# Moving the prompt's value product behind four groups of transposes in an attention stage

## The chip, the core and the metric

The kernel runs on one core of a Trainium2 chip. The metric is the device time of one launch in microseconds (us). Smaller is better. TensorE is PE in the profile, and its weight loads are listed apart as PEld; VectorE is DVE, ScalarE is ACT, GpSimd is POOL, and SP is the engine whose queue issues most transfers.

## What is computed

One inference step of a two-layer decoder: a recurrent layer (retention and a gated linear recurrence), then an attention layer, each with a SwiGLU block behind it. 1024 prompt positions and 8 samples of 8 new positions go through it together. The change lies in the attention of the second layer, which does two things:

```python
# prompt: 16 heads, 128 positions a block, keys of three dilated windows combined
s = q @ k.T * Dh ** -0.5 - slope * distance        # banded, per head
p = exp(s - max(s));  den = sum(p)
o = (p @ v) / den
# samples: 8 x 8 queries against 2048 cached keys and values of each sample, gathered by stride,
# and against the 8 new ones; same softmax, same combination
```

## The kernel before

**Slots.** The attention stage is a software pipeline of slots n, written out in one order for every engine. A slot is one block of 128 prompt queries of one pair of heads: 8 pairs (`HP`) times 8 blocks (`QT`), n = 0 to 63. In slot n TensorE makes the scores of block n (`scores(n)`, L2419), the transposes of the probabilities of block n - 1, and the value product of block n - 2 (`pv(n - 2)`, L2501 and L2505). The later the block in its pair (n % 8), the wider its scores (128 to 1024 keys) and the more there is to transpose.

**The samples ride along.** Eight slots carry one sample b: its step is s = (n + 5) % 8, so the last sample but its tail ends at slot 55. Steps 0 to 5 transpose ten tiles of cached keys (L2444) and multiply each by the sample's queries (`tile_scores`, L2472), step 6 transposes the sample's probabilities, and step 7 takes the sample's value product (L2526, L2523).

**Turns.** A group of transposes is a turn: usually four 128x128 blocks that fill one PSUM bank, then one copy out of the bank by ACT (cached keys, L2561) or DVE (probabilities, L2638). A cached key tile takes two turns. `TURN_BANK` gives four banks, numbered 0 to 3; a table made ahead of time, `TB_`, gives each turn the bank that was used longest ago of those allowed. Banks 2 and 3 are the second halves of the score banks. Where the scores of a slot are wider than 512 keys (n % 8 of 4 or more), these two are not allowed in parts 1 and 2 of the slot. `turn` waits on `t_out` until the bank's last content has been copied out.

**Parts of a slot.** A slot has four parts f. Part 1 holds the scores and turns 0 and 1, part 2 turns 2 and 3, part 3 turns 4 and 5, part 4 the rest. `SCORED` says behind which part each key tile is multiplied: tile 0 behind part 2 of step 0, tile 1 behind part 3 of step 0, tiles 2 and 3 likewise in step 1, tile 4 behind part 2 of step 2, tile 7 behind part 2 of step 4. Those four tiles behind part 2 (0, 2, 4, 7) are all made from turns 0 and 1 of the slot or from earlier ones.

For the four steps concerned the first four turns and their banks are:

```
step 0 (n % 8 = 3): key, key, key, key             banks: four different ones
step 1 (n % 8 = 4): key, key, key, key             banks: 1, 0, 1, 0
step 2 (n % 8 = 5): key, key, key, probabilities   banks: 1, 0, 1, 0
step 4 (n % 8 = 7): key, key, key, probabilities   banks: 1, 0, 1, 0
```

**The other engines.** ACT in a slot: copies out key turns 0 and 1, exponential of the first head's scores (L2585), key turn 2, exponential of the second head, key turn 3, then the row of reciprocal denominators that `pv` left in PSUM (L2607). DVE: scores plus bias with their maxima (L2679), the reciprocal (L2684), the copies of the probability turns (L2638) and of the sample's scores (L2653) in TensorE's order, last the output of `pv` times that row (L2710, semaphore `a_ox`), for which the next `pv` waits, as both use one bank. POOL makes the diagonal matrix for `pv` (L2765) and issues the loads of q, k, v and bias. SP loads the cached tiles, each buffer as soon as the turns or products that read it have run.

Of the kernel before, what the change touches and what calls it, by code (L numbers as in the profile page):

```python
# [132 lines left out]
def build(nc, a):  # L133
# [2121 lines left out]
    def slot_of(b, s):  # L2255

        return LAST_S.get(s, 8 * b + s - LEAD) if b == DB - 1 else 8 * b + s - LEAD

    def sample_slot(n):
        b, s = divmod(n + LEAD, 8)  # L2260
        if n >= min(LAST_S.values()) or b >= DB or slot_of(b, s) != n:
            b, s = DB - 1, next((s for s, x in LAST_S.items() if x == n), None)
        return (b, s) if s is not None else (None, None)

    K_AT = (0, 4, 8, 11, 14, 17, 20, 20, 20)
    SCORED = {(0, 2): (0,), (0, 3): (1,), (1, 2): (2,), (1, 3): (3,), (2, 2): (4,), (3, 1): (5,), (3, 3): (6,), (4, 2): (7,),
              (5, 1): (8,), (5, 3): (9,)}
    WEIGHED = {(7, 1): range(1, 5), (7, 2): range(5, 8), (7, 4): (8, 9, 10, 0)}

    def turns(n):  # L2270

        units = []
        b, s = sample_slot(n)
        if n == -LEAD:
            units += [("qs", 0, 0), ("ks", 0, 0)]
        if b is not None:
            units += [("k", i // 2, i % 2) for i in range(K_AT[s], K_AT[s + 1])]
        if -LEAD < n <= 2 - LEAD:
            units += [("qk", 0, 2 * (n + LEAD - 1) + i) for i in range(2)]
        elif 0 <= n < NSLOT - QT and n % QT in (1, 2):  # L2280
            units += [("qk", n // QT + 1, 2 * (n % QT - 1) + i) for i in range(2)]
        if n == slot_of(DB - 1, 7) + 3:
            units += [("out", 0, 0), ("out", 1, 0)]
        if s == 6:
            units += [("s", b, z) for z in range(3)]
        if 1 <= n <= NSLOT:
            units += [("p", n - 1, k) for k in range(0, 2 * ((n - 1) % QT + 1), 4)]
        return units
# [5 lines left out]
    def phase(n, f):  # L2294

        nt = len(turns(n))
        return range(2 * f - 2, min(2 * f, nt) if f < 4 else nt)
# [40 lines left out]
    def tile_used(j):  # L2338

        b, u = divmod(j, 20)  # L2340
        if u < 10:
            s = max(i for i in range(8) if K_AT[i] <= 2 * u + 1)
            n = 8 * b + s - LEAD
            return n, max(i for i, x in enumerate(turns(n)) if x[0] == "k" and x[1] == u)
        s, f = [x for x, steps in WEIGHED.items() if u - 9 in steps][0]
        return slot_of(b, s), 20 * f + u
# [54 lines left out]
    def att_pe(pe):  # L2401
        def scores(n):
            p, qb = divmod(n, QT)
            W = (qb + 1) * P
            if n:
                pe.wait_ge(a_red, 2 * n)
            else:
                pe.wait_ge(v_out, NT * N_QKV)
            if qb == 0:
                bank, count = qk_last(p)  # L2410
                pe.wait_ge(t_out[bank], count)
            for c in range(0, W, 512):
                if c:
                    for x in (2, 3):
                        if turns_before(n, x):
                            pe.wait_ge(t_out[x], turns_before(n, x))
                for i, (q, k) in enumerate(((QH, KH), (QH, KL), (QL, KH))):
                    for e in range(2):
                        mm = pe.matmul(PS[:, 2 * e + c // 512, 0:min(512, W - c)],  # L2419
                                       q[p % 2][e * DH:(e + 1) * DH, qb * P:(qb + 1) * P],  # L2420
                                       k[p % 2][e * DH:(e + 1) * DH, c:min(W, c + 512)], start=(i == 0), stop=(i == 2))
            mm.then_inc(a_s, 1)
# [53 lines left out]
        def tile_scores(b, t):  # L2476
            bank, count = k_last(b, t)
            pe.wait_ge(t_out[bank], count)
            if t == 0:
                pe.wait_ge(b_qb, 5 * (b + 1) + 2 if b else 6)  # L2480
                if b:
                    pe.wait_ge(b_o4, b)
            elif t % 2 == 0:
                pe.wait_ge(b_red, 6 * b + t // 2 + 1)
            mm = sample_scores(lambda hp: SKT[:, t % 2, hp, :], (t % 2) * P, P)
            if t == 1:
                mm = sample_scores(lambda hp: KNB[:, hp, :], 2 * P, DS)
            if t % 2:
                mm.then_inc(b_sc, 1)

        def pv(m):
            p, qb = divmod(m, QT)
            bank, count = last_turn(m + 1, "p", m)
            pe.wait_ge(t_out[bank], count)
            if qb == 0:
                pe.wait_ge(a_vl[p % 2], 16 * (p // 2 + 1))
            if m:
                pe.wait_ge(a_ox, m)
            for x in range(qb + 1):
                for e in range(2):  # L2500
                    pe.matmul(PS[e * DH:(e + 1) * DH, 6, 0:P], VN[p % 2][:, x, e * DH:(e + 1) * DH],  # L2501
                              PT[:, m % 2, e * (qb + 1) + x, :], start=(x == 0), stop=(x == qb), tile_position=(0, e * DH))
            pe.wait_ge(a_dg, m + 1)
            for e in range(2):
                mm = pe.matmul(PS[e * DH:(e + 1) * DH, 6, P:2 * P], ones[:, 0:DH], ADG[:, m % 2, e, :],  # L2505
                               start=True, stop=True, tile_position=(0, e * DH))
            mm.then_inc(a_o, 1)

        def sample_pv(b, steps):
            for i in steps:  # L2510
                t = i - 1
                j = 20 * b + 10 + t
                if i == 1:
                    for bank, count in last_turns(slot_of(b, 6), "s", b):
                        pe.wait_ge(t_out[bank], count)
                if i == 0:
                    pe.wait_ge(b_vn if b else b_v0, 16 * max(b, 1))
                else:
                    pe.wait_ge(b_tile[BUF[j]], load_due(j))
                for g in range(4):  # L2520
                    c = slice(256 * g, 256 * (g + 1))
                    if i == 0:
                        mm = pe.matmul(PS[NQ * g:NQ * (g + 1), 7, 256:512], PTS[0:DS, NTL, NQ * g:NQ * (g + 1)], VNB[:, c],  # L2523
                                       start=False, stop=True, tile_position=(0, NQ * g))
                    else:
                        mm = pe.matmul(PS[NQ * g:NQ * (g + 1), 7, 256:512], PTS[:, t, NQ * g:NQ * (g + 1)], TILE[BUF[j]][:, c],  # L2526
                                       start=(i == 1), stop=False, tile_position=(0, NQ * g))
                if i != NTL:
                    mm.then_inc(b_vu, 1)

        def step(n, f):
            b, s = sample_slot(n)
            if 0 <= n < NSLOT and f == 1:
                scores(n)
            for i in phase(n, f):
                turn(n, i)
            if 2 <= n and f == 1:
                pv(n - 2)
            for t in SCORED.get((s, f), ()):
                tile_scores(b, t)  # L2540
            sample_pv(b, WEIGHED.get((s, f), ()))

# [443 lines left out]
```

## Time and profile before

| | |
|---|---|
| median of 3 runs | 2783.97 us (2781.9 to 2784.48) |
| profiled execution: its own time | 2784.42 us |
| its span | 2782.6 us |
| PE busy, share of the span | 2739.0 us, 98% |
| PEld busy | 2618.6 us, 94% |
| DVE busy | 1737.1 us, 62% |
| ACT busy | 946.1 us, 34% |
| granted TensorE clock, mean | 0.998 of full speed |

The profile is one execution. The attention slots run from about 1504 to 1929 us. In rows of the timeline, the first column is the start in us from the span's start and the second the length; equal instructions are merged, with their number behind the x. In square brackets stands the idle time of the engine ahead of the row, and what ended it; "issue" means that the profile shows nothing that it waited for. Most fp32 matmuls are two instructions in the trace, a transpose is one. A 128*64 ahead of a shape is the part of the array used, rows by columns.

### The profile page before, as it was taken

How to read it: one execution, taken by the hardware profiler on the slowest of the kernel's cores; microseconds unless marked ns; L12 is line 12 of the kernel's file. 1: busy time of each engine (PE TensorE's matmuls, PEld its weight loads, DVE VectorE, ACT ScalarE, POOL GpSimd, SP SyncE). 2: the span in 40 equal slices, each digit the busy share in tenths (PEclk: the TensorE clock that was granted, in tenths of full speed). 3: DMA queues.
4: the chain of work that ended last, by engine and by line, in shares of the span. 5: the costliest groups of instructions: out<-in, count | busy, mean ns of one | idle time of the engine just before them, and what ended most of it. 6: DMA issues, size and time to landing. Idle time of an engine off the chain costs nothing.

```text
span 2782.6 us, 54662 instructions
## 1 busy us (share of the span) xinstructions
PE 2739.0 (98%) x23577; PEld 2618.6 (94%) x23577; DVE 1737.1 (62%) x2858; ACT 946.1 (34%) x1690; POOL 118.5 (4%) x220
## 2 busy tenths in 40 slices
PE   7999999999999999999999999999999999999998
PEld 7999999999999999999997777777999999999998
DVE  5754536877777776755512566556377767776676
ACT  5543513322222222422223555555232222222222
POOL 1010000000000000000011111110000000000000
PEclk9999999999999999999999999999999999999999
DMA  5120220111111111232356776873101111111112
GB/s 200 37 80 18 67 92 30 32 60 47 47 46 46 46 46 47 85 112 85 95 176 212 237 258 220 266 253 129 61 16 46 46 46 47 46 47 46 53 55 80
DMA packets 126381, 254.53 MB, mean 91 GB/s; under 512 B 7617, under 2 KB 88725, under 8 KB 125632
## 3 DMA queue, kind: packets, MB, share of 16 engines
q1 hardware_dynamic: 112944, 189.26, 21.0%
q0 software_dynamic: 11888, 57.25, 5.9%
q8 instruction: 189, 3.10, 0.5%
q10 hardware_dynamic: 1312, 4.52, 0.5%
q14 instruction: 48, 0.39, 0.0%
HBM read 222.98 MB, written 28.02 MB: 90 GB/s over the span
## 4 chain that ended last, share of the span: by engine, by line
PE 92%; DVE 4%; ACT 2%; DMA 1%; issue 1%; POOL 0%; ACTq 0%; POOLq 0%; DVEq 0%
PE psum L1574 30%; PE psum L1629 17%; PE psum L483 14%; PE psum L224 11%; PE psum L1549 3%; PE psum L2444 3%; PE psum L2501 2%; PE psum L2419 2%; PE psum L2459 2%; PE psum L2472 1%; PE psum L2526 1%; DMA x_natural<-in_x_prompt 1%; DMA cache_tile<-in_cache_k 1%; PE psum L592 1%; PE psum L2448 1%
## 5 line engine op out<-in xcount | busy, mean ns | idle before, releaser
L1810 DVE TENSOR_TENSOR x_res<-x_res,psum 128x544 f32<-128x544 f32 x352 | 250.5, 719 | 155.5 <-PE psum L1629 155.5
L483 PE MATMUL psum<-w_hi,h_hi 128*128 128x256 f32 (+1 forms) x1152 | 327.2, 284 | 1.0 <-ACT qkv_tok L2074 1.0
L483 PE MATMUL psum<-w_hi,h_lo 128*128 128x256 f32 (+1 forms) x1152 | 323.6, 281 | 0.0
L483 PE MATMUL psum<-w_lo,h_hi 128*128 128x256 f32 (+1 forms) x1152 | 323.0, 280 | 0.0
L1629 PE MATMUL psum<-ffn_hi,ffn_unit_hi 128*128 128x272 f32 x1408 | 292.6, 289 | 1.8 <-DVE x_res L1810 1.5
L1629 PE MATMUL psum<-ffn_lo,ffn_unit_hi 128*128 128x272 f32 x1408 | 291.5, 288 | 0.0
L1629 PE MATMUL psum<-ffn_hi,ffn_unit_lo 128*128 128x272 f32 x1408 | 290.7, 288 | 0.0
L1574 PE MATMUL psum<-h_hi,ffn_unit_lo 128*128 128x272 f32 x1280 | 265.2, 288 | 0.0
L1574 PE MATMUL psum<-h_lo,ffn_unit_hi 128*128 128x272 f32 x1280 | 264.8, 288 | 0.0
L1574 PE MATMUL psum<-h_hi,ffn_unit_hi 128*128 128x272 f32 x1280 | 264.5, 288 | 0.0
L1629 PEld LDWEIGHTS psum<-ffn_hi,ffn_unit_hi 128*128 128x128 f32 x1408 | 220.7, 188 | 3.2 <-DVE x_res L1810 3.2
L1629 PEld LDWEIGHTS psum<-ffn_lo,ffn_unit_hi 128*128 128x128 f32 x1408 | 220.8, 188 | 0.0
L1629 PEld LDWEIGHTS psum<-ffn_hi,ffn_unit_lo 128*128 128x128 f32 x1408 | 220.7, 188 | 0.0
L483 PEld LDWEIGHTS psum<-w_hi,h_hi 128*128 128x128 f32 (+1 forms) x1152 | 215.1, 187 | 4.6 <-issue 2.2
L483 PEld LDWEIGHTS psum<-w_lo,h_hi 128*128 128x128 f32 (+1 forms) x1152 | 215.2, 187 | 0.0
L483 PEld LDWEIGHTS psum<-w_hi,h_lo 128*128 128x128 f32 (+1 forms) x1152 | 215.0, 187 | 0.0
L1574 PEld LDWEIGHTS psum<-h_hi,ffn_unit_hi 128*128 128x128 f32 x1280 | 201.0, 188 | 0.0
L1574 PEld LDWEIGHTS psum<-h_hi,ffn_unit_lo 128*128 128x128 f32 x1280 | 200.7, 188 | 0.0
L1574 PEld LDWEIGHTS psum<-h_lo,ffn_unit_hi 128*128 128x128 f32 x1280 | 200.6, 189 | 0.0
L1574 PE MATMUL psum<-ffn_t_hi,ffn_unit_lo 128*128 128x272 f32 x960 | 198.6, 288 | 0.0
L1574 PE MATMUL psum<-ffn_t_hi,ffn_unit_hi 128*128 128x272 f32 x960 | 198.6, 288 | 0.0
L1574 PE MATMUL psum<-ffn_t_lo,ffn_unit_hi 128*128 128x272 f32 x960 | 198.5, 288 | 0.0
(385 smaller groups left out, 5307.1 us busy)
## 6 DMA issues: line engine op xcount, KB each, us to landing
cache_tile<-in_cache_k SPq DMA_DIRECT2D x64, 512.0 KB, 8.5
cache_tile<-in_cache_v SPq DMA_DIRECT2D x64, 512.0 KB, 11.9
w_raw<-in_w_ffn_gate SPq DMA_DIRECT2D x22, 1024.0 KB, 5.1
w_raw<-in_w_ffn_up SPq DMA_DIRECT2D x22, 1024.0 KB, 5.1
w_raw<-in_w_ffn_down SPq DMA_DIRECT2D x22, 1024.0 KB, 4.9
w_raw<-in_w_in_att SPq DMA_DIRECT2D x12, 1024.0 KB, 7.1
w_raw<-in_w_in_rec SPq DMA_DIRECT2D x10, 1024.0 KB, 5.0
park_x<-x_res POOLq DMA_DIRECT2D x2, 4368.0 KB, 13.3
```

What stands on the lines that cost most here:

```text
L224: mm = pe.matmul(PS[:, bank + c, 0:n], st[slot][:, wc:wc + P], mv[:, k, c * CW:c * CW + n], start=(i < NCH), stop=(i >= 3 * NCH * nk - NCH))
L483: mm = pe.matmul(PS[0:n, bank, 0:BW], st[:, k, w:w + n], mv[slot][:, k * BW:(k + 1) * BW], start=(k == 0 and x == 0) if used is None else ...
L592: pe.matmul(PS[:, bank, 0:n], wt[:, j, :], XC[j % 2][:, c * CW:c * CW + n], start=True, stop=True).then_inc(g_in, 1)
L1549: mm = pe.matmul(PS[:, 2 * s + c, 0:CC], st[slot][:, k * BW + f * P:k * BW + (f + 1) * P], mv[:, k, t * TH + c * CC:t * TH + (c + 1) * CC] ...
L1574: mm = pe.matmul(PS[:, 2 * s + c, 0:CC], st[i % NU][:, k * P:(k + 1) * P], mv[:, k0 + k, t * TH + c * CC:t * TH + (c + 1) * CC], start=(fr ...
L1629: mm = pe.matmul(PS[:, 2 * s + c, 0:CC], st[(w0 + m // 2) % NU][:, x:x + P], mv[:, f, t * TH + c * CC:t * TH + (c + 1) * CC], start=(n < 2 ...
L1810: dve.tensor_tensor(x, x, pset(dset(g, i)), ALU.add).then_inc(s_res, 1)
L2419: mm = pe.matmul(PS[:, 2 * e + c // 512, 0:min(512, W - c)], q[p % 2][e * DH:(e + 1) * DH, qb * P:(qb + 1) * P], k[p % 2][e * DH:(e + 1) * ...
L2444: mm = pe.transpose(to[:, h * P:(h + 1) * P], TILE[BUF[j]][:, hp * P:(hp + 1) * P], ident[:, :])
L2448: mm = pe.transpose(to[:, t * P:(t + 1) * P], (QN, KN)[c // 2][:, 4 * (c % 2) + t, :], ident[:, :])
L2459: mm = pe.transpose(to[:, (k - c) * P:(k - c + 1) * P], SX[x % 2][:, e, y * P:(y + 1) * P], ident[:, :])
L2501: pe.matmul(PS[e * DH:(e + 1) * DH, 6, 0:P], VN[p % 2][:, x, e * DH:(e + 1) * DH], PT[:, m % 2, e * (qb + 1) + x, :], start=(x == 0), stop ...
```

## The change

In steps 0, 1, 2 and 4 of a sample `pv(n - 2)` is issued in part 2 of the slot, behind turns 2 and 3 and directly ahead of the product of a key tile, in place of part 1, behind turns 0 and 1. In all other slots it stays in part 1. No instruction is added or taken out, and the order on the other engines and in the bank table stays.

```diff
     SCORED = {(0, 2): (0,), (0, 3): (1,), (1, 2): (2,), (1, 3): (3,), (2, 2): (4,), (3, 1): (5,), (3, 3): (6,), (4, 2): (7,),
               (5, 1): (8,), (5, 3): (9,)}
+    PV_AT = {0: 2, 1: 2, 2: 2, 4: 2}
     WEIGHED = {(7, 1): range(1, 5), (7, 2): range(5, 8), (7, 4): (8, 9, 10, 0)}
...
                 scores(n)
             for i in phase(n, f):
                 turn(n, i)
-            if 2 <= n and f == 1:
+            if 2 <= n and f == PV_AT.get(s, 1):
                 pv(n - 2)
             for t in SCORED.get((s, f), ()):
                 tile_scores(b, t)
```

Sample 0 has these steps in slots below 0, where there is no `pv`. Samples 1 to 7 have them in slots 3 to 55, four each, 28 slots in all.

## Rows read from the trace of the kernel before

**Rows 1.** The page: engine totals, and the chain that ended last.
```profile
PE 2739.0 (98%) x23577; PEld 2618.6 (94%) x23577; DVE 1737.1 (62%) x2858; ACT 946.1 (34%) x1690; POOL 118.5 (4%) x220
...
PE 92%; DVE 4%; ACT 2%; DMA 1%; issue 1%; POOL 0%; ACTq 0%; POOLq 0%; DVEq 0%
```

**Rows 2.** Waits of PEld, 1526 to 1830 us: total us, times, longest.
```profile
PEld psum L2444 <- issue: 14.9, 54, 2.9
...
PEld psum L2472 <- ACT smp_kt L2561: 2.9, 12, 0.3
PEld psum L2419 <- DVE att_pt L2638: 2.8, 6, 0.5
```

**Rows 3.** Waits of PE, same stretch.
```profile
PE psum L2444 <- DMA cache_tile<-in_cache_k: 2.5, 1, 2.5
```

**Rows 4.** Timeline of PEld, slot 12 (step 1).
```profile
1587.25 0.85 PEld L2444 LDWEIGHTS psum<-ident,cache_tile 128*128 128x128 f32 x8
1588.27 0.64 PEld L2501 LDWEIGHTS psum<-att_pt,att_v 128*64 128x64 f32 x12 [0.17 <-issue]
...
1589.30 0.85 PEld L2444 LDWEIGHTS psum<-ident,cache_tile 128*128 128x128 f32 x8 [0.17 <-issue]
1590.32 0.38 PEld L2472 LDWEIGHTS psum<-smp_kt,smp_q_blocks 128*32 128x32 f32 x16 [0.17 <-issue]
1590.89 0.85 PEld L2459 LDWEIGHTS psum<-ident,att_scores 128*128 128x128 f32 x8 [0.20 <-issue]
1591.93 0.38 PEld L2472 LDWEIGHTS psum<-smp_kt,smp_q_blocks 128*32 128x32 f32 x16 [0.18 <-ACT smp_kt L2561]
```

**Rows 5.** Timeline of ACT, slot 12.
```profile
1587.94 1.09 ACT L2561 ACTIVATE smp_kt<-psum 128x512 f32<-128x512 f32 x2 [2.43 <-PE psum L2444]
...
1589.99 0.60 ACT L2561 ACTIVATE smp_kt<-psum 128x512 f32<-128x512 f32 x1 [0.16 <-PE psum L2444]
...
1591.29 0.59 ACT L2561 ACTIVATE smp_kt<-psum 128x512 f32<-128x512 f32 x1
```

**Rows 6.** Timeline of PEld, slot 14: value product, key tile, 16 transposes, key tile.
```profile
1602.17 0.25 PEld L2505 LDWEIGHTS psum<-att_diag,ones 128*64 128x64 f32 x4
1602.59 0.38 PEld L2472 LDWEIGHTS psum<-smp_kt,smp_q_blocks 128*32 128x32 f32 x16 [0.17 <-issue]
1603.17 0.42 PEld L2444 LDWEIGHTS psum<-ident,cache_tile 128*128 128x128 f32 x4 [0.20 <-issue]
...
1605.07 0.14 PEld L2472 LDWEIGHTS psum<-smp_kt,smp_q_blocks 128*32 128x32 f32 x5 [0.17 <-issue]
```

**Rows 7.** Timeline of PEld, slot -1: three key turns, two banks, no value product.
```profile
1501.65 0.89 PEld L2444 LDWEIGHTS psum<-ident,cache_tile 128*128 128x128 f32 x8
1503.04 0.42 PEld L2444 LDWEIGHTS psum<-ident,cache_tile 128*128 128x128 f32 x4 [0.49 <-ACT smp_kt L2561]
```

**Rows 8.** Timeline of ACT, slot -1.
```profile
1502.39 1.08 ACT L2561 ACTIVATE smp_kt<-psum 128x512 f32<-128x512 f32 x2
```

**Rows 9.** Timeline of PEld, slot 11 (step 0): its first turn and its second key tile.
```profile
1581.03 0.86 PEld L2444 LDWEIGHTS psum<-ident,cache_tile 128*128 128x128 f32 x8 [0.36 <-issue]
...
1585.39 0.38 PEld L2472 LDWEIGHTS psum<-smp_kt,smp_q_blocks 128*32 128x32 f32 x16 [0.30 <-ACT smp_kt L2561]
```

**Rows 10.** Timeline of ACT, slot 11: key turn 3.
```profile
1584.76 0.58 ACT L2561 ACTIVATE smp_kt<-psum 128x512 f32<-128x512 f32 x1
```

**Rows 11.** Timeline of ACT, slot 15 (step 4): its last copy.
```profile
1612.25 0.26 ACT L2607 ACTIVATE att_rden_rows<-psum 128x128 f32<-128x128 f32 x1
```

**Rows 12.** Timeline of DVE, slot 15: end of its queue.
```profile
1612.22 1.62 DVE L2638 COPY att_pt<-psum 128x512 f32<-128x512 f32 x3
1613.76 0.28 DVE L2710 TENSOR_TENSOR att_out<-psum,att_rden_rows 128x128 f32<-128x128 f32 x1
```

**Rows 13.** Timeline of PEld: first turns of slot 15, value product of slot 16.
```profile
1607.22 0.86 PEld L2444 LDWEIGHTS psum<-ident,cache_tile 128*128 128x128 f32 x8 [0.36 <-issue]
...
1614.27 1.51 PEld L2501 LDWEIGHTS psum<-att_pt,att_v 128*64 128x64 f32 x28 [0.17 <-issue]
```

## The prediction

> **What bounds the kernel now.** I read the page first. PE is busy for 98% of the span and makes up 92% of the chain that ended last [rows 1], so whatever adds to or takes from PE's line of work should show in the time, unless PE waits for something later in the same slot. Next I asked what PE waits for in the attention slots. From 1526 to 1830 us one wait is for a transfer, 2.5 us [rows 3], and it lies ahead of the first moved product (slot 3's first turn). The waits for DVE are six of at most 0.5 us, and those for ACT are 12 of at most 0.3 us [rows 2]. The rest of PEld's idle time is put down to issue: some 0.2 us each time PE goes from full-width transposes to a product on a part of the columns or back [rows 2, 4]. PE is therefore nearly always behind its own work, and the slot's length is the sum of its PE groups plus these gaps. The reader should see in the timeline that a slot is a ladder: turns, gap, value product, gap, turns, gap, key tile, gap, turns.
>
> **What the change moves.** Nothing is added. In 28 slots the value product goes from between turns 1 and 2 to behind turn 3. I work it out from the start of turn 0 to the start of turn 4, for slot 12. Let V stand for the whole value product to the next group's start (1589.30 - 1588.27 = 1.03 us); it has the same length in both places, since the step from a value product to a key tile takes as long as that to a transpose: from L2505's first load to the next group it is 1602.59 - 1602.17 = 0.42 us [rows 6], with an idle of 0.17 us in either case [rows 4, 6].
>
> *Before* [rows 4]: turns 0 and 1 take 1588.27 - 1587.25 = 1.02 us, gap included; V; turns 2 and 3 take 1590.32 - 1589.30 = 1.02 us; the key tile takes 1590.89 - 1590.32 = 0.57 us. Sum 2.61 us + V.
>
> *After, if no bank holds PE up*: 16 transposes in a row (4 at 1603.17 and 12 behind them) with one gap take 1605.07 - 1603.17 = 1.90 us [rows 6], then V, then 0.57 us. Sum 2.47 us + V. That saves 0.14 us a slot: one gap out of four goes.
>
> *After, with the banks as they are* (steps 1, 2 and 4): turn 2 takes the bank of turn 0, and turn 3 that of turn 1. Today V lies between, and ACT has emptied both banks by 1587.94 + 1.09 = 1589.03, ahead of turn 2 at 1589.30 [rows 4, 5]. This cover goes. ACT begins the first copy 1587.94 - 1587.25 = 0.69 us after turn 0 starts, and ends both at 0.69 + 1.09 = 1.78 us. How long PE takes to go on behind a copy can be read in slot -1, which has just this order: the copies begin at 1502.39, one lasts about 0.60 us [rows 5], and turn 2 starts at 1503.04, so 0.05 us behind it, after 0.49 us of idle [rows 7, 8]. So turn 2 starts at 0.69 + 0.60 + 0.05 = 1.34 us and runs 0.42 us to 1.76. Turn 3 waits for the second copy and starts at 1.78 + 0.05 = 1.83 us. With its own 0.42 us and the gap of 0.17 us, V starts at 2.42 us. The sum is 2.42 + 0.57 = 2.99 us + V, against 2.61 us + V: **0.38 us longer** in each such slot. Put otherwise, 0.52 us of waiting is new and 0.14 us of gap is saved.
>
> Steps 2 and 4 have a probability turn as turn 3, but in the bank of turn 1, so the same copy by ACT gates it. Over all 21 slots of these three steps ACT starts its first copy 0.69 or 0.70 us after turn 0, and the two pairs of turns take 1.02 or 1.03 us each; the longer value products of steps 2 and 4 are part of V and cancel. 21 x 0.38 = 8.0 us.
>
> *Step 0* (7 slots) has four different banks, so its turns 2 and 3 don't wait, and 0.14 us is saved up to turn 4. But the slot's next key tile (tile 1) needs turn 3's copy, which ACT makes behind both exponentials: it ends at 1584.76 + 0.58 = 1585.34, and PE starts the tile at 1585.39 after 0.30 us of idle, against the 0.17 us it would have anyway [rows 9, 10]. This 0.13 us of waiting grows by what PE gained. ACT is held there by its own queue and DVE's maxima, not by the transposes. So step 0 is worth 0; if ACT moved forward too, it would be -0.14 x 7 = -1.0 us.
>
> **What hides the rest, and what is late next.** ACT's copies of turns 2 and 3 stand behind its exponentials: in slot 12 turn 3's copy ends at 1591.29 + 0.59 = 1591.88 and PE reaches tile 3 at 1591.93 with almost nothing to spare [rows 4, 5]. After the change PE comes there 0.38 us later, so this does not add. The value product's own result comes later, at 2.42 us + V in place of 1.02 us + V. ACT copies its denominator row last in the slot: in slot 15, at 1612.25 [rows 11]. There the product would have ended some 2.42 + 1.68 us after 1607.22 [rows 13] (1.68 us is V for its 24 + 4 instructions), at about 1611.3, so 0.9 us ahead of ACT, and ACT is not held. DVE's output comes last too, at 1613.76 behind its copies, and these wait for turns that all move by the same 0.38 us [rows 12]. POOL's diagonal is made in the slot before, or early in it. SP's loads of key tiles are released by turns 2 and 3, which come 2.05 - 1.34 = 0.7 us earlier in the slot; the one transfer wait stands ahead of all of it [rows 3], so this buys nothing.
>
> In slot 14 and its like PE waits up to 0.5 us for DVE's copy of a probability turn [rows 2]. That copy follows turns 4 and 5 of slot 13, which the change delays as much as the scores behind them, so the wait stays and doesn't soak up the 0.38 us.
>
> **The sum.** 21 x 0.38 + 7 x 0 = +8.0 us. The profiled execution took 2784.42 us, so it would become 2792.4 us; it lies 0.45 us above the median of the runs, and the median would become 2792.0 us (+0.29%). Against 0.2% (5.6 us), about what a measurement of this kernel tells from no change, this is slower, with not much room.
>
> **Bounds.** For the wait: nothing, as all other engines' work in these slots is hidden, up to what slot -1 shows, where turn 2 starts 1.39 us after turn 0 and not 1.34; if both waits had 0.05 us more, a slot would lose 0.48 us, or 10.1 us in all. At the low end step 0's gain is kept: 7.0 us. For lower ones see the rivals.
>
> **What a page says.** The Trainium skill, TensorEngine Tiling (Array Packing), section Key Properties, says that changing the tiling mode drains TensorE, while changing the tile alone doesn't. The trace agrees as far as it goes: the idle of 0.17 to 0.20 us stands where the part of the array changes (128*128, 128*64, 128*32) and not between transposes of two kinds [rows 4, 6]. By this rule alone the change saves one of four switches in 28 slots, and the kernel gets faster; that is the first rival, and it is worked out there from rows.
>
> **Rivals.**
> 1. *The saved switch decides (faster).* If ACT freed the banks in time, each slot would gain its gap, up to 0.17 us [rows 4]: 28 x 0.17 = 4.8 us, so 2779.2 us. For this, ACT would have to end its two copies about 0.5 us earlier than it does, by 1.25 us after turn 0's start in place of 1.78. It starts at 0.69 us in every slot, with turn 0 only just finished, and is idle ahead of that (2.43 us [rows 5]), so it can't start earlier. Chance 0.05.
> 2. *The wait is absorbed (no change that shows).* The new wait would be given back where PE waits anyway: DVE's copy of the slot behind step 2 (0.50 - 0.17 = 0.3 us, 7 times, 2 us) if DVE, which can take step 2's first probability turn earlier, came through sooner, and step 0's 1.0 us. Then 8.0 - 3.0 = +5.0 us, 2789.0 us. Against it, the copy starts when the turn is done and not when DVE is free. Chance 0.10.
> 3. *The late value product adds a wait of its own (slower still).* Its output would reach DVE late, and the next slot's product, which waits for the bank, would stand. The tightest is step 4: DVE's output ends at 1614.04 [rows 12] and the next product's first load stands at 1614.27 [rows 13]. If ACT's row slipped past its place by 0.3 us in each of the 21 slots, it would add 6 us: 2798 us. The 0.9 us of slack above speaks against it. Chance 0.06.
>
> **How the numbers follow.** The forecast, with its bounds of 7.0 to 10.1 us, has 0.79. From these bounds alone the range would be 2791.0 to 2794.1 us; with a scatter of the median of 1 to 2 us (the runs shown lie 2.6 us apart), 2789.5 to 2795.5 us. To leave out no more than 2 in 10, the range takes in rival 2 partly: 2788.0 to 2795.5 us. Slower by over 0.2% (above 2789.5 us): the forecast and rival 3, 0.84. Within 0.2%: rival 2 and the forecast's lower edge, 0.11. Faster: rival 1, 0.05.
>
> **What would show it in the profile after.** In slots of steps 1, 2 and 4, sixteen transposes ahead of L2501 with two idles of PEld put down to ACT smp_kt L2561: about 0.5 us ahead of turn 2 and less than 0.1 us ahead of turn 3, together some 11 us over 21 slots. From turn 0 to turn 4 slot 12 should take 3.64 + 0.38 = 4.02 us. In step 0, no idle ahead of turn 2, and tile 1 still at 4.36 us behind turn 0, its idle up from 0.30 to about 0.44 us. L2444's gaps put down to issue should fall by about 28 x 0.17 us. The forecast is wrong if the wait at turn 2 is absent, if ACT starts its copies sooner, or if new waits of L2501 on att_out or of L2505 on att_diag appear.

## The result and the profile after

The changed kernel took 2790.84 us (median of 13 runs, 2788.95 to 2792.08), the kernel before 2784.56 us in its 13 runs beside it. The ratio is 1.0022, with a 95% interval of 1.0015 to 1.0029: some 6.1 us slower, between 4.2 and 8.1 us. The forecast was +8.0 us, 2792.0 us, with a range of 2788.0 to 2795.5 us. Of the 27 runs of the kernel before that stand beside the last four experiments, one took 9802.58 us and is left out of their ratios. The changed file has one line more above the attention code, so L2444 of before is L2445 now, and so on.

The page of the kernel after, engine totals, and the chain that ended last, by line:

```profile
span 2788.4 us, 54662 instructions
...
PE 2740.0 (98%) x23577; PEld 2618.5 (94%) x23577; DVE 1737.4 (62%) x2858; ACT 943.7 (34%) x1690; POOL 118.8 (4%) x220
...
PE psum L1574 30%; PE psum L1629 17%; PE psum L483 14%; PE psum L224 11%; PE psum L1549 3%; PE psum L2502 2%; PE psum L2445 2%; PE psum L2420 2%; PE psum L2460 2%; PE psum L2473 2%; PE psum L2527 1%; ACT smp_kt L2562 1%; DMA x_natural<-in_x_prompt 1%; PE psum L592 1%; PE psum L2449 1%
```

The work is the same to within 1 us on PE, PEld, DVE and POOL, and 2.4 us less on ACT [rows 1]; the span is 5.8 us longer. The chain now names ACT's copy of the cached keys (`smp_kt`), which is not among the fifteen entries on the page of the kernel before. The waits of PEld from 1526 to 1838 us say where it stands:

```profile
PEld psum L2445 <- issue: 10.3, 30, 2.5
PEld psum L2473 <- issue: 9.4, 55, 0.2
PEld psum L2445 <- ACT smp_kt L2562: 8.8, 18, 0.5
...
PEld psum L2420 <- DVE att_pt L2639: 2.8, 6, 0.5
...
PEld psum L2473 <- ACT smp_kt L2562: 1.5, 5, 0.3
```

Against [rows 2]: the cached keys' transposes (L2445) have 24 gaps put down to issue less (54 to 30), and a new wait on ACT, 18 times 0.49 us (this stretch holds 18 of the 21 slots). The wait for DVE's copies is unchanged, 2.8 us.

Slot 12 (step 1), the timeline of PEld and under it that of ACT, to be laid beside [rows 4, 5]:

```profile
1588.50 0.85 PEld L2445 LDWEIGHTS psum<-ident,cache_tile 128*128 128x128 f32 x8
1589.84 0.91 PEld L2445 LDWEIGHTS psum<-ident,cache_tile 128*128 128x128 f32 x8 [0.49 <-ACT smp_kt L2562]
1590.92 0.63 PEld L2502 LDWEIGHTS psum<-att_pt,att_v 128*64 128x64 f32 x12 [0.17 <-issue]
...
1591.94 0.38 PEld L2473 LDWEIGHTS psum<-smp_kt,smp_q_blocks 128*32 128x32 f32 x16 [0.17 <-issue]
1592.52 0.86 PEld L2460 LDWEIGHTS psum<-ident,att_scores 128*128 128x128 f32 x8 [0.20 <-issue]
1593.54 0.38 PEld L2473 LDWEIGHTS psum<-smp_kt,smp_q_blocks 128*32 128x32 f32 x16 [0.17 <-issue]
```
```profile
1589.19 1.09 ACT L2562 ACTIVATE smp_kt<-psum 128x512 f32<-128x512 f32 x2 [2.43 <-PE psum L2445]
...
1590.98 0.60 ACT L2562 ACTIVATE smp_kt<-psum 128x512 f32<-128x512 f32 x1
...
1592.27 0.60 ACT L2562 ACTIVATE smp_kt<-psum 128x512 f32<-128x512 f32 x1
```

ACT starts its first copy 1589.19 - 1588.50 = 0.69 us behind turn 0, as before. Turn 2 follows 1.34 us behind turn 0. The second group of eight loads takes 0.91 us and not 0.85: the small wait ahead of turn 3 lies inside it. It is too short to be listed as idle, so the second of the two idles that the forecast named does not appear as a row. The value product starts at 2.42 us, and turn 4 at 1592.52 - 1588.50 = 4.02 us. All three are the numbers of the forecast.

Slot 11 (step 0), PEld, then ACT:

```profile
1582.43 1.73 PEld L2445 LDWEIGHTS psum<-ident,cache_tile 128*128 128x128 f32 x16 [0.36 <-issue]
1584.33 0.42 PEld L2502 LDWEIGHTS psum<-att_pt,att_v 128*64 128x64 f32 x8 [0.17 <-issue]
...
1585.71 0.64 PEld L2460 LDWEIGHTS psum<-ident,att_scores 128*128 128x128 f32 x6 [0.20 <-issue]
1586.64 0.38 PEld L2473 LDWEIGHTS psum<-smp_kt,smp_q_blocks 128*32 128x32 f32 x16 [0.29 <-ACT smp_kt L2562]
```
```profile
1584.72 0.20 ACT L2586 ACTIVATION_READ_ACCUMULATOR att_scores<-att_scores,att_max 128x1 f32 x1
1584.81 0.59 ACT L2562 ACTIVATE smp_kt<-psum 128x512 f32<-128x512 f32 x1
...
1585.99 0.60 ACT L2562 ACTIVATE smp_kt<-psum 128x512 f32<-128x512 f32 x1
```

The same slot before, turn 4:

```profile
1584.46 0.64 PEld L2459 LDWEIGHTS psum<-ident,att_scores 128*128 128x128 f32 x6 [0.20 <-issue]
```

Sixteen transposes run through without a wait, and turn 4 starts 1585.71 - 1582.43 = 3.28 us behind turn 0, in place of 1584.46 - 1581.03 = 3.43 us [rows 9]: the saved gap is 0.15 us. But tile 1 comes earlier too: it starts 1586.64 - 1582.43 = 4.21 us behind turn 0, and the forecast had it stay at 4.36 us [rows 9].

From the starts of the scores one can take the length of every slot in both traces. Slots 0 to 3, 45, 50, 51 and 53 hold pauses or waits of other kinds and are set aside (last section). In the others the differences, after less before, are these, the same within 0.02 us from sample to sample:

| step | forecast, us a slot | trace, us a slot |
|---|---|---|
| 0 | 0.00 | -0.15 |
| 1 | +0.38 | +0.36 |
| 2 | +0.38 | +0.39 |
| 4 | +0.38 | +0.37 |
| 3, 5, 6, 7 | 0.00 | 0.00 (within 0.01) |

Times seven samples, that is 7 x 0.97 = +6.8 us. The two profiled spans differ by less, 5.8 us. The rest lies in the slots set aside and ahead of slot 0 (last section).

Slot 3, the first with a moved product, is one of those set aside. PE waits there for a cached key tile, 2.5 us before and 2.1 us after, standing idle, and then runs for a few us at a lower granted clock: the mean between 1528 and 1530 us is 0.62 before and 0.50, the lower level of 1.2 GHz, after. All 16 transposes ahead of the moved product take 3.17 us there, in place of 1.73 us in slot 11.

### The profile page after: what moved, and what is told of

It reads as the page before. It is cut to its first block, busy times and chain, and to the rows that moved or that the text cites. A ratio compares the mean times of both kernels' runs of the same rounds, so it can differ in the third digit from the quotient of the medians.

```text
span 2788.4 us, 54662 instructions
## 1 busy us (share of the span) xinstructions
PE 2740.0 (98%) x23577; PEld 2618.5 (94%) x23577; DVE 1737.4 (62%) x2858; ACT 943.7 (34%) x1690; POOL 118.8 (4%) x220
## 4 chain that ended last, share of the span: by engine, by line
PE 92%; DVE 4%; ACT 3%; DMA 1%; issue 1%; POOL 0%; ACTq 0%; POOLq 0%; DVEq 0%
PE psum L1574 30%; PE psum L1629 17%; PE psum L483 14%; PE psum L224 11%; PE psum L1549 3%; PE psum L2502 2%; PE psum L2445 2%; PE psum L2420 2%; PE psum L2460 2%; PE psum L2473 2%; PE psum L2527 1%; ACT smp_kt L2562 1%; DMA x_natural<-in_x_prompt 1%; PE psum L592 1%; PE psum L2449 1%
```

## The experiments

A difference "a slot" is always against the kernel before, taken from the starts of the scores as above, in the samples that hold no such pause. The medians of the first four experiments stand beside 2784.01 us for the kernel before, those of the last four beside 2784.27 us. The ratios differ from the quotient of the two medians by up to 0.0006. Lines that a diff leaves out are marked by "..."; `PV_AT = {0: 2}` and the short copies are shown against the changed kernel, ACT's new order against the run ahead of it, the others against the kernel before.

### The move in step 0 alone

```diff
-    PV_AT = {0: 2, 1: 2, 2: 2, 4: 2}
+    PV_AT = {0: 2}
```

> The product moves in step 0 alone (7 slots, four different banks, so no wait for a bank). Theory A, read from the profile after: the third key copy of ACT starts 0.15 us sooner there because its transposes come sooner, the rest of ACT's chain follows, and each of the 7 slots gets 0.15 us shorter: -1.0 us in all, about 2783.5 us against 2784.6, and no wait on ACT ahead of turn 2. Theory B, as the prediction had it: tile 1 is held by ACT anyway, the slots keep their length, 0.0 us. The time can hardly tell them apart, the starts of the slots in the trace can (5.93 us from slot 11 to slot 12 before, by B the same, by A 5.78).

Measured: 2784.22 us against 2784.01 us, ratio 0.9999 (0.9991 to 1.0008), no difference that the time can tell. The trace can: five samples have step 0 shorter by 0.14 or 0.15 us, every other step without a pause is within 0.02 us. Slot 27, PEld:

```profile
1688.79 1.73 PEld L2445 LDWEIGHTS psum<-ident,cache_tile 128*128 128x128 f32 x16 [0.37 <-issue]
...
1693.00 0.38 PEld L2473 LDWEIGHTS psum<-smp_kt,smp_q_blocks 128*32 128x32 f32 x16 [0.30 <-ACT smp_kt L2562]
```

Again 4.21 us and not 4.36. Theory A holds, and the forecast's zero for step 0 does not. The reason can be seen in ACT's timeline of slot 11 in the kernel before, in two rows that the forecast did not use:

```profile
1583.32 0.20 ACT L2585 ACTIVATION_READ_ACCUMULATOR att_scores<-att_scores,att_max 128x1 f32 x1
1583.56 0.60 ACT L2561 ACTIVATE smp_kt<-psum 128x512 f32<-128x512 f32 x1
```

The third copy starts 0.24 us behind the row ahead of it. Where only ACT's own queue holds such a copy it starts 0.09 us behind (1584.72 to 1584.81 after the change). It was waiting for turn 2's transposes, for too short a time to be listed as idle. They come sooner now, the copy starts 2.38 us behind turn 0 in place of 2.53, and everything behind it on ACT moves along, tile 1 too. From there ACT's own queue holds the copy, so these 0.15 us are all that a slot of step 0 can gain while ACT keeps its order. That PE's saved gap is 0.15 us as well is a coincidence; the run with two tiles side by side, further down, tells the two apart.

### The tile moved up to the product

The product stays behind turn 1, and tiles 0, 2, 4 and 7 are multiplied directly behind it, in samples 1 to 7. `scored` takes the place of `SCORED.get((s, f), ())` on PE and DVE, here and in every later run whose edit names `EARLY`.

```diff
+    EARLY = {0: 1, 2: 1, 4: 1, 7: 1}
+
+    def scored(b, s, f):
+        if not b:
+            return SCORED.get((s, f), ())
+        return [t for (x, g), ts in SCORED.items() for t in ts if x == s and EARLY.get(t, g) == f]
...
-            for t in SCORED.get((s, f), ()):
+            for t in scored(b, s, f):
```

> Product and key tile stand side by side as in the changed kernel, but the tile moves up to the product (behind turn 1), not the product down to the tile. Theory A (ACT's copies decide, a change of array part costs 0.15 us): no wait for a bank ahead of turn 2, but turns 2 and 3 come 0.57 us later. In steps 0 and 1 ACT's third copy waits for them, and with it the second key tile: +0.6 us and +0.57 us a slot. In step 2 DVE's copies come a little late for the second half of the next scores: +0.1. In step 4 nothing waits: -0.14. Sum 7 x 1.1 = +8 us, 2792.5 us. Theory C (it is the neighbourhood that pays, and the loss came from moving the product late): every one of the 28 slots gets 0.14 us shorter, -4 us, 2780.6 us.

Measured: 2792.59 us, ratio 1.0028 (1.0016 to 1.0039). Slot 28 (step 1), PEld, then ACT:

```profile
1698.89 0.86 PEld L2451 LDWEIGHTS psum<-ident,cache_tile 128*128 128x128 f32 x8
...
1700.94 0.38 PEld L2479 LDWEIGHTS psum<-smp_kt,smp_q_blocks 128*32 128x32 f32 x16 [0.17 <-issue]
1701.52 0.86 PEld L2451 LDWEIGHTS psum<-ident,cache_tile 128*128 128x128 f32 x8 [0.20 <-issue]
1702.34 0.90 PEld L2466 LDWEIGHTS psum<-ident,att_scores 128*128 128x128 f32 x8
1704.16 0.38 PEld L2479 LDWEIGHTS psum<-smp_kt,smp_q_blocks 128*32 128x32 f32 x16 [0.91 <-ACT smp_kt L2568]
```
```profile
1702.21 0.60 ACT L2568 ACTIVATE smp_kt<-psum 128x512 f32<-128x512 f32 x1 [0.73 <-PE psum L2451]
1702.71 0.82 ACT L2592 ACTIVATE att_scores<-att_scores,att_max 128x640 f32<-128x640 f32 x1
...
1703.52 0.59 ACT L2568 ACTIVATE smp_kt<-psum 128x512 f32<-128x512 f32 x1
```

In slot 11 (step 0) even the first key tile waits for ACT's copy, 0.17 us longer than the usual gap:

```profile
1585.24 0.41 PEld L2479 LDWEIGHTS psum<-smp_kt,smp_q_blocks 128*32 128x32 f32 x16 [0.34 <-ACT smp_kt L2568]
```

No turn waits for a bank here, one change of the array part less is made, and the kernel is as slow as the changed one. Turns 2 and 3 come late, ACT's third copy waits 0.73 us for them, and its fourth copy holds tile 3 for 0.91 us. By slot: step 0 +0.77, step 1 +0.58, step 2 -0.15, step 3 +0.15 (DVE's copies of step 2 come late for the second half of the scores), step 4 -0.15, step 5 +0.07. In step 5 the product starts 1.06 us behind turn 0 in place of 1.02, and DVE's output, which frees its bank, ends 0.11 us ahead of it in place of 0.23 us; that the late output is the cause was not tried. The sum of 7 x 1.27 = 8.9 us was forecast as 8 us; step 0 was under-estimated, because tile 0 itself waits for ACT there. Theory C, that the neighbourhood pays, would have given 28 slots of -0.14 us, and falls.

### Short copies

The changed kernel, with ACT copying 128 of 512 columns of turns 0 and 1 in steps 1, 2 and 4. Three quarters of those key tiles are left uncopied.

```diff
+            w = 1 if n % QT in (4, 5, 7) and n > 0 and i < 2 else 4
-            act.activation(SKT[:, x % 2, 4 * c:4 * c + 4, :].rearrange("p a w -> p (a w)"), bank,
+            act.activation(SKT[:, x % 2, 4 * c:4 * c + w, :].rearrange("p a w -> p (a w)"), bank[:, 0:w * P],
```

> The changed kernel, but ACT copies only 128 of the 512 columns of turns 0 and 1 in steps 1, 2 and 4; three quarters of those key tiles are not copied. Theory A (turns 2 and 3 wait for ACT to empty the two banks): the first copy then takes some 0.27 us in place of 0.60, turn 2 starts at 0.69 + 0.27 + 0.05 = 1.01 us behind turn 0 in place of 1.34, turn 3 at about 1.44, and the product at 2.03 in place of 2.42. 21 x 0.39 = 8 us come off the changed kernel: about 2783 us, 1 us below the kernel before. Theory C (the loss comes from the product being late, whatever ACT does): about 2791 us as the changed kernel.

Measured: 2782.44 us, ratio to the kernel before 0.9997 (0.9988 to 1.0006), against 1.0022 with full copies. Slot 28, PEld, then ACT:

```profile
1693.22 0.86 PEld L2445 LDWEIGHTS psum<-ident,cache_tile 128*128 128x128 f32 x8
1694.24 0.86 PEld L2445 LDWEIGHTS psum<-ident,cache_tile 128*128 128x128 f32 x8 [0.17 <-ACT smp_kt L2563]
1695.27 0.64 PEld L2502 LDWEIGHTS psum<-att_pt,att_v 128*64 128x64 f32 x12 [0.17 <-issue]
```
```profile
1693.91 0.28 ACT L2563 ACTIVATE smp_kt<-psum 128x128 f32<-128x128 f32 x1 [2.44 <-PE psum L2445]
```

With a copy of 0.28 us turn 2 starts 1.02 us behind turn 0 (forecast 1.01) and the product 2.05 us (forecast 2.03). Steps 1, 2 and 4 are back at the length of before within 0.02 us, though the product still stands behind turn 3. The 0.17 us that turn 2 still waits use up the gap that is saved. So the loss against the kernel before is the wait for ACT's copies, and no cost of the late product itself is left over.

### Pairs taken apart

In steps 3 and 5 tiles 5 and 8 stand beside the product in the kernel before. Here they move behind turns 2 and 3.

```diff
+    EARLY = {5: 2, 8: 2}
```

> The kernel before, but where product and key tile stand side by side already (tile 5 in step 3, tile 8 in step 5, 14 slots) the tile moves behind turns 2 and 3, so that TensorE changes the part of the array once more. Theory A (a change costs 0.14 to 0.17 us wherever it is): the 14 slots get 0.14 us longer each, +2.0 us, 2786.6 us, seen in the starts of the slots. Rival D (the gap is only the wait for the last result and is hidden or not depending on what follows): the slots keep their length within 0.03 us, 0 us.

Measured: 2786.0 us against 2784.01 us, ratio 1.0006 (0.9997 to 1.0015); this interval does not exclude no change. In the trace each of the seven slots of step 3 is 0.14 or 0.15 us longer, each of step 5 from slot 8 on too, 14 slots and 2.0 us in all as forecast; all others but those set aside 0.00 (within 0.02). Rival D falls. Slot 30 shows four gaps where there were three:

```profile
1709.29 1.07 PEld L2508 LDWEIGHTS psum<-att_pt,att_v 128*64 128x64 f32 x20 [0.17 <-issue]
...
1710.75 0.42 PEld L2451 LDWEIGHTS psum<-ident,cache_tile 128*128 128x128 f32 x4 [0.17 <-issue]
...
1711.77 0.38 PEld L2479 LDWEIGHTS psum<-smp_kt,smp_q_blocks 128*32 128x32 f32 x16 [0.17 <-issue]
1712.35 0.86 PEld L2466 LDWEIGHTS psum<-ident,att_scores 128*128 128x128 f32 x8 [0.20 <-issue]
```

One more change of the array part is thus worth 0.15 us here too, taken away or added. The Trainium skill, TensorEngine Tiling (Array Packing), section Key Properties, says that changing the tiling mode drains TensorE. The gaps of 0.17 and 0.20 us above agree with that; that a drain is what fills them, no run here shows. Nor does every change of the part show as idle: between the scores, on 64*128, and the first turn of slot 12 none is listed [rows 4].

### Two tiles side by side, ACT's order as it was

If a change of the part costs 0.15 us and waits come from ACT's order, a better arrangement can be worked out. In steps 0 and 1 both key tiles are multiplied at the end of the slot, and in step 0 the product stands ahead of them, behind six groups of transposes.

```diff
+    PV_AT = {0: 3}
+    EARLY = {0: 3, 2: 3}
```

> Steps 0 and 1: tiles 0 and 1 side by side at the end of the slot, tiles 2 and 3 likewise, and in step 0 the product ahead of them behind six groups of transposes; ACT's order as it was. TensorE changes the part of the array twice less in steps 0 and 1, and no turn waits for a bank (in step 1 the product stays between turns 1 and 2). By the count of changes alone (0.15 us each, as measured): 14 slots x 0.30 = -4.2 us. By theory A, ACT's fourth copy still stands behind its second exponential and holds the second tile of the pair: step 0 as with the moved product, -0.15 us, step 1 0.0 us; sum -1.0 us, 2783 us, with the idle on ACT ahead of the second tile up to 0.3 us and more.

Measured: 2782.18 us, ratio 0.9998 (0.9989 to 1.0007). Step 0 is 0.15 us shorter, step 1 unchanged. Slot 28, its last rows on PEld:

```profile
1697.38 0.38 PEld L2480 LDWEIGHTS psum<-smp_kt,smp_q_blocks 128*32 128x32 f32 x16 [0.17 <-issue]
1698.12 0.38 PEld L2480 LDWEIGHTS psum<-smp_kt,smp_q_blocks 128*32 128x32 f32 x16 [0.36 <-ACT smp_kt L2569]
```

Two changes of the part fewer in 14 slots bring next to nothing: what is saved turns into a longer wait for ACT's fourth copy, as theory A had it. In step 0 PE saves two changes and the slot is still only 0.15 us shorter: the limit is ACT's queue, as worked out above.

### The same with ACT's fourth copy ahead of its second exponential

```diff
-            for i in mine[2:3]:
+            cut = 4 if s in (0, 1) else 3
+            for i in mine[2:cut]:
...
-            for i in mine[3:]:
+            for i in mine[cut:]:
```

> As the one before, and ACT makes its fourth copy ahead of its second exponential in steps 0 and 1. Theory A: the wait on ACT ahead of the second tile goes; step 0 from turn 0 to tile 1 is 2.54 + 0.80 + 0.40 = 3.74 us in place of 4.36 (-0.62), step 1 4.33 in place of 4.69 (-0.36). Sum 7 x 0.98 = -6.9 us, about 2777.5 us. If ACT does not matter, the same time as the run before.

Measured: 2778.86 us, ratio 0.9981 (0.9972 to 0.9990). Step 0 is 0.56 us shorter, step 1 0.29 or 0.30 us, some 0.06 us less each than forecast; why was not looked into. In slot 28 both tiles run as one group:

```profile
1695.54 0.81 PEld L2480 LDWEIGHTS psum<-smp_kt,smp_q_blocks 128*32 128x32 f32 x32 [0.17 <-ACT smp_kt L2569]
1696.55 0.19 PEld L2427 LDWEIGHTS psum<-att_k_hi,att_q_hi 64*128 64x128 f32 x2 [0.20 <-issue]
```

PE's order is that of the run before; ACT's order alone makes the step from 0.9998 to 0.9981, in the trace from -0.15 to -0.56 us in step 0 and from 0.00 to -0.29 us in step 1.

### Tiles 4, 7 and 9 last in their slots

```diff
+    EARLY = {4: 3, 7: 4, 9: 4}
```

> Steps 2, 4 and 5: tiles 4, 7 and 9 as the last thing of their slots, directly ahead of the next scores; all else as before. One change of the array part less in each of 21 slots, 0.15 us (0.17 in step 5). In step 2 DVE's copies also end earlier against the second half of the next scores, whose wait of 0.44 us (0.17 of it there anyway) goes: -0.27 more. Sum 7 x (0.42 + 0.15 + 0.17) = -5.2 us, about 2779 us. A rival: in step 4 DVE's output comes later than the next product wants its bank (0.2 us of slack before), which would cost some tenths a slot and eat this step's gain.

Measured: 2779.4 us, ratio 0.9984 (0.9975 to 0.9992). Step 2 -0.15 us, the following step 3 -0.27 or -0.36 us in turn (the wait on DVE's copy, 0.44 or 0.50 us in turn before, is gone), step 4 -0.15, step 5 -0.15. The rival of a late output in step 4 does not show. Behind the last sample's step 5 a late output does show once: the product of slot 57 waits 0.60 us for DVE's output in place of 0.33 us, and the slot is 0.26 us longer.

### Both

The edits of the last two runs together: `PV_AT = {0: 3}`, `EARLY = {0: 3, 2: 3, 4: 3, 7: 4, 9: 4}`, and ACT's order.

> Both of the last two together. Theory A: the terms add, -6.9 - 5.2 = -12.1 us, about 2772.5 us, as no term uses the other's slack. If PE's time were bound by something outside these slots, less.

Measured: 2772.82 us against 2784.27 us, ratio 0.9961 (0.9947 to 0.9974). That is 10.9 us (7.2 to 14.8) faster than the kernel before. The terms add: the steps of a sample come to -0.56, -0.30, -0.14, -0.32, -0.14 and -0.14 us for steps 0 to 5, 1.6 us a sample or 11.2 us in all, against 12.1 us forecast. This kernel beats both the one before and the changed one.

## Why the prediction was right, point by point

**The bound.** Right: PE's line of work sets these slots. Every difference in a slot's length could be read from PE's groups, gaps and waits.

**The new wait for two banks.** Right in kind, place and size: turn 2 at 1.34 us, the product at 2.42 us, turn 4 at 4.02 us. The short copies show that it is the cause, not only that it is there.

**The saved gap.** Right: 0.14 us forecast, 0.15 us measured up to turn 4 of step 0, and 0.15 us a slot in five other places (steps 3 and 5 taken apart, steps 2, 4 and 5 joined).

**Step 0.** This is the term that was mis-sized: 0.0 us forecast, -0.15 us measured, -1.0 us over seven slots. The failing step was the sentence that ACT is held there by its own queue and DVE's maxima, not by the transposes. Its third copy was held by the transposes, by some 0.15 us that no row listed as idle. The alternative was priced at -1.0 us in the forecast, but not taken. That the price came out exactly is in part luck: it was PE's gap, and what ACT could give was another 0.15 us.

**The rivals.** The first (the saved switch decides) did happen in step 0, the only step with four banks, and nowhere else. The second (the wait is absorbed) named two places: DVE's copy behind step 2 soaked up nothing, as argued (six waits, 2.8 us, before and after), and step 0's 1.0 us was the error above. The third (a late value product) had no trace: no wait on `att_out` of the next product appears among the waits from 1526 to 1838 us, and the short copies leave no room for it.

**The transfers.** The forecast said that the one wait for a transfer stands ahead of all moved products. Its rows end at 1830 us and miss a second one, at turn 2 of slot 51, a slot of step 0. It is there in both kernels (last section), and slot 51 gained nothing where the undisturbed slots of step 0 gained 0.15 us.

**The sum.** 7 x (0.36 + 0.39 + 0.37 - 0.15) = +6.8 us by the slots, +6.1 us (4.2 to 8.1) by the timed runs, +8.0 us forecast. The corrected step 0 accounts for most of the difference between forecast and slots. Both measured sums lie below the 7.0 us that the forecast gave as the low end of its mechanism, though the interval of the timed runs takes it in; the range that was stated went further down for scatter and for a part of the second rival.

## What to carry to other kernels

A block of work between two users of the same buffer is cover, whatever else it is. Before moving it, lay the release of the buffer (here 1.34 and 1.83 us behind the first user) beside the time at which the next user would arrive without it (about 0.87 and 1.30 us, estimated from the 1.73 us that sixteen transposes take in step 0). To save one switch of 0.15 us does not pay where it uncovers a wait of 0.5 us, and where another engine's order ends the slot, two saved switches bring nothing until that order is changed too. And a wait can be hidden in a row with no idle listed: compare its distance to the row ahead with that of the same pair elsewhere.

## What was unexpected

The slots repeat to 0.01 or 0.02 us from sample to sample, so that a term of 0.15 us a slot, below what the timed runs can tell, can be read from a single trace. Against this stand single pauses that PEld's rows put down to issue. Three between 1530 and 1870 us in the kernel before:

```profile
1807.78 0.74 PEld L2501 LDWEIGHTS psum<-att_pt,att_v 128*64 128x64 f32 x13 [0.64 <-issue]
...
1849.71 0.85 PEld L2444 LDWEIGHTS psum<-ident,cache_tile 128*128 128x128 f32 x8 [0.59 <-issue]
...
1865.01 0.64 PEld L2459 LDWEIGHTS psum<-ident,att_scores 128*128 128x128 f32 x6 [0.74 <-issue]
```

The kernel after has one such row in the same stretch:

```profile
1854.18 0.86 PEld L2445 LDWEIGHTS psum<-ident,cache_tile 128*128 128x128 f32 x8 [0.72 <-issue]
```

The second of before and the one of after both stand ahead of turn 2 of slot 51, and there PE's own rows name what PEld's do not, the transfer of a cached key tile. Before, then after:

```profile
1849.75 1.06 PE L2444 MATMUL psum<-ident,cache_tile 128*128 128x128 f32 x8 [0.38 <-DMA cache_tile<-in_cache_k]
```
```profile
1854.21 1.07 PE L2445 MATMUL psum<-ident,cache_tile 128*128 128x128 f32 x8 [0.51 <-DMA cache_tile<-in_cache_k]
```

So "issue" on PEld does not mean that nothing was waited for; PE's rows of the same moment have to be read too. The other two, in slots 45 and 53, are put down to issue by PE's rows as well. What causes them was not tried and stays open.

Slots 45 and 53 are together 1.4 us shorter after than the table would make them. Slots 0 to 3, 50 and 51 are together 0.7 us longer than that, and the start of slot 0 lies 0.3 us earlier. Together with the table's 6.8 us that gives the 5.8 us between the spans.
